# A two-block model on one core: the first feed-forward part on unscaled activations, and value products of the second attention ahead of their factor

## The reference

```python
# end of the first block: norm, modulation, feed-forward part with a convolution over tokens
x = x_mid + g2 * conv_ffn(rms_norm(x_mid, norm2_w) * (1 + sc2) + sh2, w_up, conv_w, conv_b, w_down)

def conv_ffn(h, w_up, conv_w, conv_b, w_down):
    u = h @ w_up                                  # 256 x 5632: two halves of 2816
    up = jnp.pad(u, ((0, 0), (1, 1), (0, 0)))     # zero before the first and behind the last token
    acc = conv_b
    for j in range(3):
        acc = acc + up[:, j:j + L] * conv_w[j]
    a, g = jnp.split(acc, 2, axis=-1)
    return (jax.nn.silu(g) * a) @ w_down

# start of the second block: 8 forgetting heads and 8 stick-breaking heads
xn = rms_norm_2(x, attn_norm)
proj = xn @ attn_w_in                             # q, k, v and 8 forget logits
```

## Time and profile before

| what | value |
|---|---|
| median of 3 runs | 1256.01 us (1255.02 to 1256.34) |
| profiled execution | 1251.87 us, of which the span is 1250.0 us |
| TensorE busy | 1235.3 us (99%), 8373 products |
| DVE, ScalarE, GpSimd busy | 725.3, 679.0, 713.2 us |
| products L555 (512 columns), L557 | 1024 each |
| read from memory | 206.01 MB |

### The profile page before, as it was taken

The page is one execution under the profiler, slowest core; times in us unless marked ns, Lnnn a source line. Parts: engine busy times, 40 slices in busy tenths (PEclk is TensorE's granted clock), DMA queues, the critical chain, the costliest instruction groups (busy, mean ns, idle before and its releaser), DMA issues.

```text
span 1250.0 us, 23623 instructions
## 1 busy us (share of the span) xinstructions
PE 1235.3 (99%) x8373; PEld 1092.6 (87%) x8373; DVE 725.3 (58%) x1574; ACT 679.0 (54%) x1232; POOL 713.2 (57%) x308
## 2 busy tenths in 40 slices
PE   7999999999999999999999999999999999999998
PEld 4788889877799799998888779999999999999998
DVE  5796667456522555555515663766666324766665
ACT  6332334455544666666645636666666445666663
POOL 5476553342268555657495406655675986665563
PEclk9999999999999999999999999999999999999999
DMA  9978542231146354556364203544554654554451
GB/s 338 370 256 304 200 154 68 88 110 57 36 134 185 119 184 171 200 183 219 112 189 149 85 18 118 186 177 176 201 205 137 199 185 145 176 201 176 176 216 54
DMA packets 58187, 208.09 MB, mean 166 GB/s; under 512 B 6640, under 2 KB 7808, under 8 KB 58112
## 3 DMA queue, kind: packets, MB, share of 16 engines
q1 hardware_dynamic: 57888, 206.56, 48.5%
q0 software_dynamic: 224, 0.52, 0.1%
HBM read 206.01 MB, written 1.05 MB: 166 GB/s over the span
## 4 chain that ended last, share of the span: by engine, by line
PE 91%; DVE 4%; ACT 2%; issue 1%; DMA 1%; POOL 0%; SPq 0%; DVEq 0%; ACTq 0%
PE ps L555 18%; PE ps L526 15%; PE ps L527 15%; PE ps L528 15%; PE ps L557 9%; PE ps L805 2%; PE ps L580 2%; PE ps L583 2%; PE ps L582 2%; PE ps L610 1%; PE ps L876 1%; PE ps L902 1%; PE ps L891 1%; ACT whi L1264 1%; DMA X<-in_xc 1%
## 5 line engine op out<-in xcount | busy, mean ns | idle before, releaser
L333 POOL TENSOR_TENSOR wlo<-raw,whi 128x1024 fp32r<-128x1024 f32 x287 | 696.7, 2442 | 508.4 <-ACT whi L1264 485.3
L1264 ACT ACTIVATE whi<-raw 128x1024 fp32r<-128x1024 f32 x338 | 352.6, 1053 | 74.9 <-DMA raw<-in_stream 36.8
L555 PE MATMUL ps<-H,whi 128*128 128x512 f32 x1024 | 364.9, 399 | 1.4 <-DVE H L1812 1.2
L557 PE MATMUL ps<-H,wlo 128*128 128x256 f32 x1024 | 287.5, 281 | 0.0
L526 PE MATMUL ps<-H,whi 128*128 128x256 f32 (+2 forms) x960 | 285.6, 298 | 1.4 <-DVE H L1783 1.1
L527 PE MATMUL ps<-H,whi 128*128 128x256 f32 (+2 forms) x960 | 277.5, 289 | 0.0
L528 PE MATMUL ps<-H,wlo 128*128 128x256 f32 (+2 forms) x960 | 277.3, 289 | 0.0
L555 PEld LDWEIGHTS ps<-H,whi 128*128 128x128 f32 x1024 | 192.5, 188 | 48.4 <-DVE H L1812 3.3
L526 PEld LDWEIGHTS ps<-H,whi 128*128 128x128 f32 (+1 forms) x960 | 183.3, 191 | 13.6 <-issue 9.8
L557 PEld LDWEIGHTS ps<-H,wlo 128*128 128x128 f32 x1024 | 193.5, 189 | 0.0
L2176 DVE SCALAR_TENSOR_TENSOR arena<-ps,sm,arena 128x255 f32<-128x255 f32 (+1 forms) x264 | 127.3, 483 | 103.7 <-ACT arena L1533 96.2
(11 more groups left out here) (328 smaller groups left out, 1484.4 us busy)
## 6 DMA issues: line engine op xcount, KB each, us to landing
raw<-in_stream SPq DMA_DIRECT2D x386, 512.0 KB, 4.1
X<-in_xc SPq DMA_DIRECT2D x4, 512.0 KB, 6.1
out_y<-X SPq DMA_DIRECT2D x8, 128.0 KB, 1.9
kx<-in_const SPq DMA_DIRECT2D x1, 512.0 KB, 8.6
params<-in_params SPq DMA_DIRECT2D x1, 344.0 KB, 6.5
kx<-in_const POOLq DMA_DIRECT2D x1, 256.0 KB, 4.4
k<-in_const POOLq DMA_DIRECT2D x1, 129.0 KB, 5.5
k<-in_const SPq DMA_DIRECT2D x1, 128.0 KB, 6.1
```

The source lines that it names most:

```text
L333: pool.tensor_tensor(wlo[:, slot, :], raw[:, rslot, :], whi[:, slot, :].bitcast(f32), ALU.subtract).then_inc(rest_done[0], 1)
L555: pe.matmul(PS[:, bank, :], wh_, F[:, k, :, :].rearrange("p h n -> p (h n)"), start=k == 0, stop=False, skip_group_check=True)
L557: mm = pe.matmul(PS[:, bank, T:2 * T], wl_, Fh[:, k, :], start=False, stop=k == KC - 1, skip_group_check=True)
L1264: act.activation(whi[:, s % RING, :], raw[:, r % RING, :], ACT.Copy).then_inc(hi_done, 1)
```

## The change

At both places with `norm(n)` the scaled activations are no longer made ahead of the first product.

First feed-forward part: it takes the form with unscaled activations. The shift does not pass through a factor that is applied later, so it goes into columns of its own: the operands `Uh` and `Ul` have 258 columns, the first and last of which hold the negated shift of the modulation. Times the up weights they give minus what the shift adds to every token. The up products become `mm3` products of 258 columns in place of `product_halves`; DVE scales the 256 middle columns by `n_r`; the convolution reads one column to the left and to the right, so that at both ends it meets the negated shift column, which stands for the zero padding; and the bias of each hidden feature is made from the first column with a new table (minus the sum of the three taps, `taps1`), one column per half and step (`bias1`). The table, `sc2` and the shift columns are made while the mixing's products run (DVE at i = 1, 2, 3 and 4, ScalarE at i = 7).

Second attention: the value products run on the split of X times the norm's weight (`Vh`, `Vl`), in banks 4 to 7, with the square sums behind the first of them. The factor is turned to a column by two products of two columns in all (`rcol`, at the seventh value block), and the four copies of the values multiply by it. The scaled activations for projections and forget gates are made meanwhile, in banks 1 to 3. The first two projections use banks 2 and 3. GpSimd waits with the third block's rest until the value operands are made. ScalarE instead of DVE fills the operands of the forgetting attention (`fox_operands`, behind the fourth projection), in other buffers. `keep_running` is gone.

```diff
-LATE_STARTS = {S_FFN2 + 2: 3, S_CONV + 2: 4, S_FFN3 + 2: 5}
+LATE_STARTS = {S_FFN1 + 2: 1, S_FFN2 + 2: 3, S_CONV + 2: 4, S_FFN3 + 2: 5}
...
+                    if s == S_ATT2 + 2:
+                        pool.wait_ge(S["vl_done"], KC)
...
+        EXT = T + 2
+        Uh, Ul = (H[:, KC * EXT * i:KC * EXT * (i + 1)].rearrange("p (k n) -> p k n", k=KC) for i in range(2))
...
-            return f == S_FFN1 or i > 0
+            return f != S_FFN1 and i > 0
...
-        LATE = 3
+        LATE = 1
...
-                            product_t(s, PS[:, 4 + 2 * (i % 2) + j, 0:T], 0, T, norm if j == 0 else None)
+                            n = EXT if f == S_FFN1 else T
+                            product_t(s, PS[:, 4 + 2 * (i % 2) + j, 0:n], 0, n, norm if (i, j) == (0, 0) else None)
...
-            sumsq(1)
-            keep_running(S_FFN1, 32)
             ffn(S_FFN1, 1)
-            sumsq(2)
-            keep_running(S_ATT2, 31)
...
             for k in range(KC):
                 wait_rest(pe, S_ATT2 + k)
-                product_n(S_ATT2 + k, D, k, lambda half: [(tt, (PS[:, 2 * tt + half, :], True)) for tt in range(2)],
-                          norm=2)
+                pe.wait_ge(S["vl_done"], k + 1)
+                product_n(S_ATT2 + k, D, k, lambda half: [(tt, (PS[:, 4 + 2 * tt + half, :], True)) for tt in range(2)],
+                          Vh, Vl)
+                if k == 0:
+                    sumsq(2)
+                if k == RCOL_AT:
+                    pe.wait_ge(S["small"], 3)
+                    for tt in range(2):
+                        mm = pe.matmul(PS[:, 0, tt:tt + 1], n_r[:, P * tt:P * tt + P], ident[:, 0:1],
+                                       start=True, stop=True)
+                    mm.then_inc(S["rc_ps"], 1)
...
-            norm(1, lambda u: MODB[:, 8 + u:9 + u])
+            norm_late(1, lambda k: sc2[:, k:k + 1])
             ffn(S_FFN1)
...
-            norm(2)
+            act.preload_act_table_set("natural_log_exp_and_others")
+            for k in range(KC):
+                act.wait_ge(S["x_ready"], 8 + k + 1)
+                act.activation(Vh[:, k, :], X[:, k, 0:T], ACT.Copy, scale=pr("anorm", k, k + 1)).then_inc(S["vh_done"], 1)
+                act.activation(sq[:, k, 0:T], X[:, k, 0:T], ACT.Square).then_inc(S["sq_ready"], 1)
+            splits_upto(S_ATT2 + RING)
+            rsqrt_start(2)
+            for u in range(KC):
+                act.wait_ge(S["h32_done"], 16 + u + 1)
+                act.activation(Fh[:, u, :], PS[:, 1 + u % 3, 0:T], ACT.Copy).then_inc(S["hh_done"], 1)
+                if u % 2 == 1:
+                    splits_upto(S_ATT2 + RING + u // 2)
...
+                            if f == S_FFN1:
+                                dve.wait_ge(S["cw_copy"], v(copies + i + 1, 2))
+                                dve.tensor_scalar(bias1[:, slot, jj:jj + 1], bank[:, 0:1],
+                                                  cwb1[:, slot, 8 + jj:9 + jj], cwb1[:, slot, 6 + jj:7 + jj],
+                                                  ALU.mult, ALU.add).then_inc(S["bias1"], 1)
+                            dve.tensor_tensor(uu_, uu_, n_r[:, 0:T], ALU.mult).then_inc(S["scaled"], 1)
...
-                            parts = ((1, T, 0), (0, T - 1, 1))
+                            parts = ((0, T, 0), (0, T, 2))
...
-            add_to_x(1, S_FFN1 - 1, lambda k: MODB[:, k:k + 1])
...
-            norm(1, lambda u: sc2[:, u:u + 1], lambda u: MODB[:, 8 + u:9 + u])
+            add_and_norm_late(1, S_FFN1 - 1, lambda k: sc2[:, k:k + 1], lambda k: MODB[:, k:k + 1])
             ffn(S_FFN1)
...
-            for bank in range(4):
-                dve.tensor_copy(v2[:, bank // 2, 512 * (bank % 2):512 * (bank % 2) + 512], PS[:, bank, :])\
-                   .then_inc(S["evac_v"], 1)
+            for n in range(4):
+                dve.tensor_scalar(v2[:, n // 2, 512 * (n % 2):512 * (n % 2) + 512], PS[:, 4 + n, :],
+                                  rcol[:, n // 2:n // 2 + 1], None, ALU.mult).then_inc(S["evac_v"], 1)
```

More of the change, by code:

```diff
@@ L564, in product_halves, with product_n @@
                     sumsq(norm, KC - 2, KC)
-            def product_n(s, width, k0, at, norm=None):
+            def product_n(s, width, k0, at, hi=Hh, lo=Hl):
                 for c in range(D // width):
                     k = k0 + c
-                    if norm is not None:
-                        pe.wait_ge(S["hl_done"], HU[norm] + k + 1)
                     wide = min(width, 512)
@@ L1481, in _ @@
                    .then_inc(S["down_hi"], 1)
+                if i == KC - 1:
+                    act.wait_ge(S["modb_done"], 1)
+                    for out in (shift_ps, Uh[:, :, 0:EXT:EXT - 1]):
+                        act.activation(out, MODB[:, 8:16].unsqueeze(2).broadcast_to((P, KC, 2)), ACT.Copy,
+                                       scale=-1.0).then_inc(S["shift_hi"], 1)
                 splits_upto(up_block(S_BRANCH, 2, KC, i, 1) + RING)
@@ L1488, in norm_late @@
                     act.wait_ge(S["x_ready"], 8 * (n - 1) + k + 1)
-                    act.activation(Fh[:, k, :], X[:, k, 0:T], ACT.Copy, scale=scale(k)).then_inc(S["hh_done"], 1)
+                    out = Uh[:, k, 1:T + 1] if n == 1 else Fh[:, k, :]
+                    act.activation(out, X[:, k, 0:T], ACT.Copy, scale=scale(k)).then_inc(S["hh_done"], 1)
                     act.activation(sq[:, k, 0:T], X[:, k, 0:T], ACT.Square).then_inc(S["sq_ready"], 1)
@@ L1494, in norm_late @@
                 rsqrt_start(n)
-            def norm(n, shift=None):
-                act.preload_act_table_set("natural_log_exp_and_others")
-                squares(n)
-                rsqrt_start(n)
-                for u in range(KC):
-                    norm_hi(n, u, None if shift is None else shift(u))
             def ffn(f):
@@ L1584, in _, with fox_operands @@
                     heads = slice(at + 4 * i, at + 4 * i + 4)
-                    spread = act.activation(spread2[i][at:at + 8, :].rearrange("r (h d) -> r h d", d=HD),
-                                            ident[at:at + 8, heads].unsqueeze(2).broadcast_to((8, 4, HD)), ACT.Copy)
-            spread.then_inc(S["heads_ready"], 1)
-            for k in range(KC):
-                splits_upto(S_ATT2 + k + RING)
+                    act.activation(spread2[i][at:at + 8, :].rearrange("r (h d) -> r h d", d=HD),
+                                   ident[at:at + 8, heads].unsqueeze(2).broadcast_to((8, 4, HD)), ACT.Copy)\
+                       .then_inc(S["heads_ready"], 1)
+            splits_upto(S_ATT2 + KC + RING - 1)
+            def fox_operands():
+                for out in (cfk, cfq, selr):
+                    act.activation(out, K0[:, 0:out.shape[1]], ACT.Copy, scale=0.0).then_inc(S["heads_clear"], 1)
+                act.activation(identr, ident, ACT.Copy).then_inc(S["heads_ready"], 1)
+                act.activation(maskr, maskA, ACT.Copy).then_inc(S["heads_ready"], 1)
+                act.wait_ge(S["heads_clear"], 9)
+                for rows in (slice(0, 8), slice(32, 40)):
+                    act.activation(selr[rows, :], ident[rows, rows], ACT.Copy).then_inc(S["heads_ready"], 1)
             def sb_logs(h):
@@ L2104, in add_to_x, with add_and_norm_late @@
                            .then_inc(done, 1)
-            def add_and_norm_late(n, last, scale):
-                if n != 4:
+            def add_and_norm_late(n, last, scale, gate=None):
+                if n in (3, 5):
                     for i in range(2):
```

194 lines of the change are left out of this document (107 added, 87 removed).

## The result

Eight executions of the changed kernel take 1243.02 to 1248.88 us, median 1243.94; eight of the kernel before 1251.14 to 1256.34, median 1253.75. The ratio of the runs is 0.9935, interval 0.992 to 0.995: faster, by 8 us. (The two medians themselves lie 9.8 us apart: in either kernel they also depend on how many executions met a lower clock, which is the subject of the next lines.) On the median that the prediction started from this is 0.9935 x 1256.01 = 1247.8 us.

What follows compares the result with a forecast made beforehand. TensorE, busy 99% of the 1250.0 us span, bounds the kernel. Terms -7.1 + 3.15 - 0.25 + 0.2 - 4.3 = -8.3 took the profiled 1251.87 us to 1243.6 and the median 1256.01 to 1247.7; range 1245 to 1252.

Steps and rivals of the forecast that it cites:

- Start of the first feed-forward part: Last mixing product to third up block: 16.35 us becomes 9.23 without dummies, -7.1 us; operand lateness taken as 0.
- The up blocks themselves: First feed-forward part: 258 columns in three products make a block 2.90 us instead of 2.825; 42 blocks cost +3.15 us.
- First down product: First feed-forward part: TensorE's idle time ahead of it falls from 0.61 to 0.35 us, -0.25 us.
- Tail and what is left of the part: End of the first feed-forward part: chain grows 0.3 a step, blocks 0.15; +0.2 us (0 to 0.5).
- Start of the second attention: First projection comes 25.85 us after the start instead of 30.16, value blocks following the last down product at once; -4.3 us.
- The slower add: Start of first feed-forward part: DVE's gated add takes 0.06 us a row more, sixth chunk about 0.4 us later.
- GpSimd's hold: First feed-forward part's start: waiting until the last operand costs nothing; third block ready near 415, wanted at 419.2.
- The chain: ScalarE and DVE work behind up products: 7.7 us a step, at most 8.2, still hidden by the 8.68 us step.
- a new wait in the dummies' place: Rival at both starts: GpSimd's hold, ScalarE's list or DVE's add takes back 3.8 to 5.7 us; chance 0.12.
- issued in two pieces: Rival in 44 up blocks: 258-column products pay 13 ns more each, 13.7 us; 0.07 together with a chain outgrowing its step.
- The clock falls without the dummies: Rival at both starts: 1.2 GHz over square sums and first value block costs about 6 us, 1253.7; chance 0.03.

Runs made afterwards that it cites:

- the paired version: Changed kernel plus forgetting-attention fillers, first two up blocks fed chunk by chunk in turn, ScalarE scaling two products before weight splits; 1242.31 to 1242.67 us, ratio 0.9913.
- fox_filled: Changed kernel with six unused 256-column products in TensorE's 0.76 us idle stretch in the forgetting attention; 1242.3 to 1244.3 us in 12 executions, ratio 0.9921.
- after_again: The changed kernel itself run once more, nothing altered, five executions; ratio to the kernel before 0.9918 (0.99 to 0.9935).
- att2_only: Second attention's start as changed, first feed-forward part as in the kernel before; ratio 0.9958 (0.9945 to 0.997), undisturbed median 1247.20 us.

## Why the prediction was right, step by step

The forecast of 1243.6 us for the profiled conditions stands against 1243.21 undisturbed, the 1247.7 against 1247.8. The mechanism of every large term was right. That the sum comes out to a few tenths is partly luck: the start of the first part saved 0.6 us less than forecast, the up blocks and the tail cost 0.8 less. Its terms:

| step of the prediction | predicted | measured |
|---|---|---|
| Start of the first feed-forward part | -7.1 | 9.81 - 16.35 = -6.5 |
| The up blocks themselves | +3.15 | 21 steps x 0.13 = +2.7 |
| First down product | -0.25 | 0.51 - 0.61 = -0.1 |
| Tail and what is left of the part | +0.2 | -0.1, as the rest of 195.44 - 199.52 |
| Start of the second attention | -4.3 | 25.72 - 30.16 = -4.4 |
| sum | -8.3 | -8.5; undisturbed times -8.3 |

*Start of the first part.* The mechanism was right, the pace of the operands was not free: 9.81 - 9.23 = 0.58 us are lost, where the prediction took 0 of its bounds of 0 to 1. TensorE waits for the fifth and sixth chunk; the low part of the sixth is ready at 411.69, and TensorE could use it at 409.47 + 5 x 0.36 = 411.27. The slower add, of which the prediction spoke, would not have been enough. What it left out stands at the first subtraction (DVE and GpSimd of the changed kernel, then the same place of the third part before):

```profile
406.62 1.13 DVE L2151 SCALAR_TENSOR_TENSOR H<-X,sm,H 128x256 fp32r<-128x256 f32 x1 [0.32 <-ACT H L1504]
...
411.22 0.47 DVE L2151 SCALAR_TENSOR_TENSOR H<-X,sm,H 128x256 fp32r<-128x256 f32 x1
```

```profile
397.94 9.53 POOL L333 TENSOR_TENSOR wlo<-raw,whi 128x1024 fp32r<-128x1024 f32 x4 [1.49 <-ACT whi L1283]
```

```profile
1052.15 0.48 DVE L2120 SCALAR_TENSOR_TENSOR H<-X,params,H 128x256 fp32r<-128x256 f32 x1 [0.31 <-ACT H L1489]
```

It meets the last of four passes of GpSimd, which the hold does not cover, and ends 0.28 us behind it, as in the kernel without holds; it takes 0.66 us longer than the others, and all later chunks come that much later. An estimate from these rows: 0.66 us earlier the sixth operand is there at 411.03, in time. No run here moves that pass; the paired version, in which a chunk lasts TensorE twice as long, gets most of the loss back although its first subtraction is as slow (1.12 us).

*GpSimd's hold.* "Costs nothing" fits the trace, in which no product waits for GpSimd there, but it was only asked what the hold delays, not what it keeps away. It is a condition of the gain: without it this part brings nothing. The third part, from which the start was taken over, has such a hold as well, and the prediction read its pace without asking what made it.

*Up blocks.* A block of 258 columns came out at 5.783 / 2 = 2.89 us (2.90 predicted), but by two errors that cancel: two columns cost 1.9 ns a product, not 0.8, and 256 columns in that place 118.6 ns, not 120. The 120 was read rightly, from a down block (2.879 us on the mean of the loop before), and carried over to the up blocks, where it does not hold. Of the 0.5 us between 3.15 and 2.7, 0.3 is that hundredth of a microsecond in 42 blocks, and 0.2 a down block that became as much shorter (2.879 to 2.870), which the prediction did not expect.

*The chain.* Still hidden behind the products: the step is 8.65 us (8.68 predicted), and it shrinks with the products in the version of 256 columns. At the end of the part the gap even shrank, from 0.26 to 0.13 us, where 0.2 more was predicted.

*Rivals.* Of a new wait in the dummies' place there are the 0.58 us above, not 3.8 to 5.7; products are not issued in two pieces. "The clock falls without the dummies" is refuted for both starts, where the clock is at 1.00, but the clock does fall elsewhere in both kernels, dummies or not, and this rival was argued from a single execution that happened to be undisturbed.

## What to carry to other kernels

A wait that a change adds should be priced both ways: what it delays, and which other engine's operations it keeps out of each other's way. A price that is multiplied a thousand times is to be read in the place where it will be paid, with one thing changed, over the period of a loop; the same product cost 118.6 ns in one kind of block and 119.4 in another. And where executions of the same kernel differ by a few microseconds, compare the mean clock first and look for the place in a trace that caught the fall: here six unused products in a short idle stretch among small products took the kernel before from a median of 1255.35 to 1251.75 us.

## What was not expected of the hardware

The granted clock fell behind an idle stretch of 0.76 us, in which TensorE came from a stage of many small products, and stayed at 0.50 for 13 us although TensorE was recorded busy throughout. There are falls at other places too, and not all have an idle stretch ahead. In the profiled execution of fox_filled there is one in the first microseconds, where TensorE idles much. In that of after_again (and of att2_only) there is one in the mixing, with TensorE recorded busy throughout; ahead of it stand four products with only 4 rows, from 227.56 to 229.5 us. In fox_filled and after_again the first up block comes at 410.9 instead of 409.47, 1.4 us later, and they take 1244.2 us. The windows of the one, then that row and the window of the other:

```profile
5.00:10.00 5.00, 2.86 (x6) 0.89 (x6) 1.38 (x2) 2.70 (x5) 0.00 (x0) 0.77 0.98 363
10.00:15.00 5.00, 4.77 (x22) 1.34 (x22) 1.84 (x4) 4.37 (x11) 1.68 (x1) 0.89 1.03 419
```

```profile
227.56 1.98 PE L867 MATMUL ps<-rows,kx 4*128 4x512 f32 x4
```

```profile
230.00:235.00 5.00, 5.00 (x27) 4.44 (x27) 4.68 (x12) 4.88 (x10) 0.00 (x0) 0.66 0.00 0
```
